# The last unit of two up-projections: sum columns multiplied apart

## The reference

```
mod = silu(c) @ w_mod[i] + b_mod[i];  sh1, sc1, g1, sh2, sc2, g2 = split(mod, 6)
h = rmsnorm(x, norm_mlp[i]) * (1 + sc2) + sh2
x = x + g2 * (relu(h @ w_up[i]) ** 2) @ w_down[i]        # w_up 1024x4096, w_down 4096x1024
```

## Time and profile before

| what | value |
|---|---|
| median of 3 runs | 1027.24 us (1024.03 to 1027.44) |
| profiled execution | 1026.5 us |
| its span | 1024.6 us |
| granted TensorE clock, mean | 0.985 |
| PE busy | 989.0 us, 7850 matmuls |
| DVE, ACT busy | 776.7 us, 545.1 us |
| HBM read | 220.13 MB |

### The profile page before, as it was taken

How to read it: one execution, slowest core, us unless ns; L and a number is a source line. 1 busy time by engine, 2 the same in 40 slices (tenths; PEclk the granted TensorE clock), 3 DMA queues, 4 the chain that set the end, 5 groups by cost and what they waited for, 6 DMA issues and landing times.

```text
span 1024.6 us, 19866 instructions
## 1 busy us (share of the span) xinstructions
PE 989.0 (97%) x7850; PEld 938.0 (92%) x7850; DVE 776.7 (76%) x1381; ACT 545.1 (53%) x897; POOL 1.9 (0%) x14
## 2 busy tenths in 40 slices
PE   4799999999999999999999999999999999999996
PEld 1479999999989899999999989898889999999996
DVE  4757976888767777668766889899987887777554
ACT  4248675444655568875544535468116565444343
POOL 0000000000000000000000000000000000000000
PEclk9689999999999999999999999999999999999998
DMA  9997797887464865554655336363445555555631
GB/s 378 421 420 308 280 372 306 310 329 274 132 204 114 304 247 179 192 170 160 213 202 200 125 127 243 112 223 122 162 162 196 178 178 200 198 177 192 205 125 42
DMA packets 35881, 222.29 MB, mean 217 GB/s; under 512 B 3883, under 2 KB 9180, under 8 KB 9436
## 3 DMA queue, kind: packets, MB, share of 16 engines
q1 hardware_dynamic: 35804, 221.22, 59.9%
HBM read 220.13 MB, written 1.07 MB: 216 GB/s over the span
## 4 chain that ended last, share of the span: by engine, by line
PE 88%; DVE 4%; ACT 3%; DMA 3%; issue 1%; SPq 0%; DVEq 0%; ACTq 0%
PE bank L595 23%; PE bank L601 22%; PE bank L596 22%; PE bank L927 11%; PE bank L976 3%; PE s_banks L624 2%; DMA mod_raw<-w_mod 1%; DVE w_lo L1408 1%; ACT w_hi L1047 1%; PE s_banks L976 1%; DMA raw<-weights 1%; DVE mod_raw L1459 1%; ACT ub L1148 1%; PE s_banks L595 0%; PE s_banks L596 0%
## 5 line engine op out<-in xcount | busy, mean ns | idle before, releaser
L1408 DVE TENSOR_TENSOR w_lo<-raw,w_hi 128x1024 fp32r<-128x1024 f32 x268 | 324.9, 1218 | 32.3 <-ACT w_hi L1047 29.9
L1047 ACT ACTIVATE w_hi<-raw 128x1024 fp32r<-128x1024 f32 x268 | 280.0, 1051 | 109.4 <-PE bank L601 103.1
L595 PE MATMUL bank<-xg_hi,w_hi 128*128 128x258 f32 (+1 forms) x1248 | 310.8, 286 | 1.3 <-DVE w_lo L1408 0.8
L596 PE MATMUL bank<-xg_lo,w_hi 128*128 128x258 f32 (+1 forms) x1248 | 306.2, 282 | 0.0
L595 PEld LDWEIGHTS bank<-xg_hi,w_hi 128*128 128x128 f32 x1248 | 236.1, 189 | 6.2 <-issue 5.1
L596 PEld LDWEIGHTS bank<-xg_lo,w_hi 128*128 128x128 f32 x1248 | 236.5, 190 | 0.2
L601 PE MATMUL bank<-xg_hi,w_lo 128*128 128x258 f32 (+1 forms) x1248 | 181.2, 283 | 0.3 <-DVE w_lo L1408 0.3
L601 PEld LDWEIGHTS bank<-xg_hi,w_lo 128*128 128x128 f32 x1248 | 162.9, 190 | 0.8 <-DVE w_lo L1408 0.8
L595 PE MATMUL bank<-hid_hi,w_hi 128*128 128x256 f32 x512 | 123.5, 279 | 0.0
L596 PE MATMUL bank<-hid_lo,w_hi 128*128 128x256 f32 x512 | 123.4, 279 | 0.0
L1811 DVE SCALAR_TENSOR_TENSOR y<-u,vec,y 128x256 f32<-128x256 f32 x240 | 98.5, 480 | 0.2
(11 more groups left out here) (238 smaller groups left out, 1259.5 us busy)
## 6 DMA issues: line engine op xcount, KB each, us to landing
raw<-weights SPq DMA_DIRECT2D x157, 1024.0 KB, 5.0
mod_raw<-w_mod SPq DMA_DIRECT2D x28, 1024.0 KB, 11.5
mod_raw<-w_dots SPq DMA_DIRECT2D x20, 1024.0 KB, 8.6
toep<-bias_by_distance SPq DMA_DIRECT2D x8, 256.0 KB, 5.4
x<-x_in SPq DMA_DIRECT2D x1, 1024.0 KB, 5.0
toep<-bias_by_distance SPq DMA_DIRECT2D x8, 128.0 KB, 3.9
y_out<-yout SPq DMA_DIRECT2D x4, 256.0 KB, 2.5
c_all<-c_row SPq DMA_DIRECT2D x1, 512.0 KB, 14.6
```

Source lines behind the costliest of these rows:

```text
L595: pe.matmul(dst, hi, r_hi, start=start, stop=False, skip_group_check=True)
L596: pe.matmul(dst, hi, r_lo, start=False, stop=False, skip_group_check=True)
L1047: act.activation(pool_w_hi[:, at, :] if name == "pool" and at < 2 else w_hi[:, at % HL, :], raw[:, slot, (at % 2) * UT * P:(at % 2 + 1) * ...
L1408: ve.tensor_tensor(lo, raw[:, slot, (at % 2) * UT * P:(at % 2 + 1) * UT * P], hi.bitcast(F32), ALU.subtract).then_inc(lo_done, 1)
```

## The change

The last unit of up0 and of up1 (unit 31) is done by a function of its own, `last_up`. In up0 the 16 matmuls by high weights keep 258 columns; the 8 by low weights are done first for the two sum columns alone and then for the 256 others. In up1 all 24 are first done for the sum columns, and then all 24 for the others, and the wait for the low weights stands ahead of them all. The last matmul raises the count, as before. For that, up1's loop of eight units runs once, and seven units behind it are written out.

```diff
--- before.py
+++ after.py
@@ -771,6 +771,28 @@
                     mm = by_low(dst[:, 0:n], (U0[name] + j) % HL, k, r_hi[:, k, 0:n], k == DC - 1)
                 mm.then_inc(pe_units, 1)
 
+            def last_up(name, i, j):
+
+                high_ready(name, i, j)
+                bank_free(name, i, j)
+                dst, slot = out_bank(name, j), (U0[name] + j) % HL
+                main, sums = slice(0, SEQ), slice(SEQ, SEQ + 2)
+                if name == "up0":
+                    for k in range(DC):
+                        by_high(dst[:, 0:SEQ + 2], slot, k, xg_hi[:, k, 0:SEQ + 2], xg_lo[:, k, 0:SEQ + 2], k == 0)
+                    low_ready(name, i, j)
+                    for k in range(DC):
+                        by_low(dst[:, sums], slot, k, xg_hi[:, k, sums], k == DC - 1)
+                else:
+                    low_ready(name, i, j)
+                    for k in range(DC):
+                        product(dst[:, sums], slot, k, xg_hi[:, k, sums], xg_lo[:, k, sums], k == 0, k == DC - 1)
+                    for k in range(DC):
+                        by_high(dst[:, main], slot, k, xg_hi[:, k, main], xg_lo[:, k, main], k == 0)
+                for k in range(DC):
+                    mm = by_low(dst[:, main], slot, k, xg_hi[:, k, main], k == DC - 1)
+                mm.then_inc(pe_units, 1)
+
             def down(name, i, j):
                 high_ready(name, i, j)
                 base = 0 if name == "down0" else 32
@@ -810,15 +832,18 @@
                     if isinstance(i, int):
                         mod_work(name, 8 * i + j)
 
-                unrolled = 32 if name == "up0" else 16
+                unrolled = 31 if name == "up0" else 16
                 if name == "up1":
                     first_two(name, xg_hi, xg_lo, SEQ + 2, (xg_lo_done, 16), lambda: stats((acc_done, 26), acc))
                 for v in range(4 if name == "up0" else 2, unrolled):
                     step(v // 8, v % 8)
                 if name == "up1":
-                    with pe.Fori(2, 4) as i:
+                    with pe.Fori(2, 3) as i:
                         for j in range(8):
                             step(i, j)
+                    for j in range(7):
+                        step(3, j)
+                last_up(name, 3, 7)
 
             up_phase("up0")
             first_down("down0")
```

## The result

The changed kernel took 1031.51 us (median of 7 runs, 1029.71 to 1032.73) against 1027.44 us for the kernel before beside it (7 runs, 1024.03 to 1029.36). The ratio is 1.0043, 95% interval 1.0032 to 1.0055. The change makes the kernel slower by 0.43%, less than the half per cent that was called "no change", and the forecast of 1030.2 us within 1026 to 1034 held.

A forecast was written before the change was run, and what follows sets the result against it. PE, busy 97% of the span, was taken as the bound. 32 narrow matmuls at 0.11 us, less 0.08 for narrower wide ones, gave +3.4 us: 1029.9 from the profiled execution, 1030.6 from the median, called 1030.2, range 1026 to 1034.

The forecast's parts named there:

- The price of a tiny matmul: Last units of up0 and up1: each of 32 added 2-column matmuls costs its weight load, 0.11 us, 3.5 us in all.
- Cheap tinies: Rival, both last units: each narrow matmul costs 0.07 us or less, +2.2 us down to 0.8, about 1028.4; chance 0.12.
- The chain on one place: Rival, both last units: each narrow matmul waits for the sum ahead of it, +8.1 us, 1034.6 us; chance 0.07.
- The moved wait and the loop: Up1: the earlier wait for low weights is met 4.0 us ahead, and the written-out loop has no price; both cost nothing.
- What follows PE: Behind both last units: eviction, relu, squares and weight refill come later by as much as PE, 0.9 and 2.6 us.
- The clock: Rival: up1's 2.6 us of narrow matmuls draw a fall to 1.2 GHz for 10 us, +4.4 us, 1034.3 us; chance 0.05.
- The range: Whole kernel: 1026 to 1034 us around 1030.2, from the main case widened by run scatter up to where dear cases begin.
- The direct terms: PE's added time in the two last units: 0.9 us in up0 and 2.6 in up1, together +3.4 us.

The follow-up runs named there:

- The halved weights: The change, with up1's 24 narrow matmuls loading only 64 of the 128 weight columns; 1026.86 us (one run).
- the cut into halves: The change, with the columns cut into 130 and 128 instead of 2 and 256, in both places; 1032.31 us (one run).
- the code alone: The kernel before, with up1's loop run once and its last eight units written out, no narrow matmuls; 1027.04 us, ratio 0.9998.
- the five sets: The change, with the 24 narrow matmuls of up1's last unit done five times over; 1052.72 us (one run).
- narrowed matmuls: The kernel before, with high-weight by low-activation matmuls 256 instead of 258 columns wide in up0, the attention's projections and up1; 1026.53 us, ratio 0.9998.
- the change twice: The changed kernel itself, measured and profiled on two occasions; 1031.51 us, ratio 1.0043, and 1031.31 us, ratio 1.0050.
- up0 only: The kernel before with only up0's part of the change, up1 keeping its loop; 1027.81 us, ratio 1.0014.
- all of up0: The change, with the low matmuls' sums done apart in units 4 to 31 of up0, not just the last; 1050.70 us, ratio 1.0238.
- all of up1: The change, with the sums done apart in units 2 to 31 of up1, not just the last; 1158.35 us, ratio 1.1287.
- up1 only: The kernel before with only up1's part of the change, up0 as before; 1030.34 us, ratio 1.0031.

## Why the prediction was right

**The price of a tiny matmul** was 0.11 us, from the four of line 640. Measured: 0.111 in both places, and the sum 0.87 + 2.61 = 3.48 against 0.9 + 2.6 - 0.08 = 3.4. The halved weights show that it is the load; the cut into halves shows that 2, 128 and 130 columns cost the same.

**Cheap tinies** failed: 0.111 us each, and 0.056 with 64 weight columns. The Trainium skill, TensorE: Matmul & The Clock Gate, section "Back-to-back issue gap", has some 25 ns for a matmul of this width. The same section gives that as the gap of a matmul by itself and says that it holds no time for weight loads, so the prediction was wrong to set it against the price. No run here had narrow matmuls without a load, so none tests the figure.

**The chain on one place** failed: 0.11 apart at a record of 0.25 us, and no less to another bank between wide ones.

**The moved wait and the loop** cost nothing that could be seen, as put: no wait for low weights in the profile after, and a ratio of 0.9998 with the code alone.

**What follows PE** moved with it: the eviction of unit 31 came 3.61 us later than before, by what down1 was later, and no wait went or came but 0.6 us in the attention.

**The clock** is the term that I mis-sized. I put it as a rival with a chance of 0.05 and +4.4 us, on top of a sum that would hold otherwise. The runs show it as a smaller thing that happens sometimes: 1 of 4 profiles, +1.5 us where it fell. I had priced it by the 10 us stretch of the earlier trace rows; the stretch was 3.4 us here. An average of 0.4 us would go some way from the direct 3.5 to the measured 4.1 and 4.6 us, but both intervals (1.0032 to 1.0055, 1.0034 to 1.0065) also hold 3.5 us, and the two kinds of scatter described at the end are larger, so this is an argument and not shown. My reason against it, that the clock had kept 1.00 at 344 to 352 us, was one execution's: in another it fell there. That the busy row of PE does not speak against a fall is shown: it was full in the five sets and the clock at 0.50. The Trainium skill, TensorE: Matmul & The Clock Gate, section "HAM oscillation — how this bites in real kernels", speaks of idle gaps between bursts. The five sets show a fall with no gap in PE's row (busy 8.70 of 8.70 us ahead of it).

**The range**: 1026 to 1034 held 1031.51. My number was low by 1.3 us, of which 0.2 is the kernel before (1027.44 beside this one, 1027.24 shown) and 0.4 that I started between the profiled execution and the median; from the median the sum was 1030.6. The direct terms were right to 0.1 us; that the total came as near, with a scatter of some 5 us in single runs, is in part luck.

## What to carry to other kernels

Price a matmul that you split off by its weight load, not by its columns: find a place in the trace where a narrow one stands with the same weights and take its distance from start to start, not its record. A split is cheap once and dear in a loop, and a long run of narrow ones was followed by a lower clock though PE was busy all the time; look for the spacing of the matmuls behind it. Change the count of a suspected cost two- and fivefold: what is proportional shows its price, and what is not shows itself.

## What the hardware showed that I had not expected

The clock fell in the middle of an unbroken stream of matmuls. At the lower level the load of 128 weight columns takes 0.214 us and a 256-column matmul also 0.214, where at full clock they are 0.111 and 0.1175. With 24 narrow and 24 wide ones in turn the mean over 200.8 us of up1 was 0.74.

The same matmul of 256 columns has two paces at the same granted clock. In the last weight phase, from the chains of the kernel before and of the one with narrowed matmuls, where that phase is the same code:

```profile
1010.94 0.91 PE bank L601 x8
...
1013.66 0.92 PE bank L601 x8
```
```profile
1010.63 0.94 PE bank L601 x8
...
1013.46 0.95 PE bank L601 x8
```

A unit takes 2.72 us in the one and 2.83 in the other, 113 and 118 ns for each of 24 matmuls. Over the phase that is 2.3 us. Eight of the fourteen profiles have the quicker pace there (before, the change twice, up0 only, written out, half weights, all of up0, all of up1) and six the slower, with no pattern that I could find in what was changed. The down phases of the two layers always ran at 118.

There is a second such difference at the start. The same four matmuls of line 640 that stand at 166.38 before and at 166.14 after stand 2 us earlier in the profile of up1 only, though nothing ahead of them was changed:

```profile
164.37 0.51 PE L640 MATMUL s_banks<-pick,mod_row 128*128 128x4 f32 x4
```

All profiles but that of all of up0, which is changed ahead of this place, fall into two groups there, near 166 (165.6 to 166.5) and near 164 us (164.0 to 164.4). The profiles before and after the change are in the same group both times, so their spans can be laid side by side. The two differences make 4 us of the scatter of some 5 us between runs of one kernel; their causes stay open.
